# One chip kernel of three network blocks: chunk buffers cleared and gate rows split one stage earlier, woven pieces placed at lone steps, a head norm inverted on one tile, and attention probabilities scaled in their turn over

## The reference, cut to what matters

```python
# first block, diff_attention: 4 heads, 4 query blocks of 128
p = jax.nn.softmax(s, axis=-1)
p = p[:, :, 0] - lam * p[:, :, 1]
return jnp.einsum('bhqk,bkhd->bqhd', p, v)

# third block, gated_delta_rule, by chunks
lmat = jnp.where(strict, jnp.einsum('bhncd,bhnsd->bhncs', kb, k) * decay, 0.0)
sol = lax.linalg.triangular_solve(lmat + eye, rhs, left_side=True, lower=True, unit_diagonal=True)
value, k_cumdecay = sol[..., :dv], sol[..., dv:]
attn_intra = jnp.einsum('bhncd,bhnsd->bhncs', q, k) * decay
# a scan over the chunks with these follows, and then
o_gdn = rms_norm(o_gdn, gdn_norm_w) * jax.nn.silu(z)
gate = jax.nn.sigmoid(gates + gate_bias)          # gates: 2048 columns of h @ w_in
return (g_fox * y_fox + g_gdn * y_gdn) @ w_out
```

## Time and profile before

| | us |
|---|---|
| median of 3 runs | 2835.96 |
| lowest, highest | 2828.89, 2838.26 |
| the profiled execution | 2823.42 |
| its span | 2822.1 |
| TensorE busy in it | 2705.8 |

### The profile page before, as it was taken

One profiled execution on the slowest core, in us unless ns is written; L12 is line 12 of the kernel. 1 busy time (PEld: TensorE's weight loads), 2 busy tenths in 40 slices (PEclk: granted clock), 3 DMA queues, 4 the chain that ended last, 5 costly groups with the idle time before them and its releaser, 6 DMA issues. The chain is left out here.

```text
span 2822.1 us, 42499 instructions
## 1 busy us (share of the span) xinstructions
PE 2705.8 (96%) x16586; PEld 2320.4 (82%) x16586; DVE 1598.9 (57%) x2482; ACT 1053.2 (37%) x1827; POOL 642.0 (23%) x509
## 2 busy tenths in 40 slices
PE   8989999999999999998999999999899989999998
PEld 6769876788888777877888888986799889999987
DVE  5875657366653455954533337965544465666643
ACT  4364333442222333353423224546434243422223
POOL 3440101221100123441100003346344320112101
PEclk9999899999999999999999999999999999999999
DMA  4200231122222321312222222210111032222221
GB/s 163 92 8 8 91 104 60 46 90 97 97 97 97 117 75 62 103 38 74 92 97 97 97 97 76 87 50 1 51 35 46 28 120 85 88 91 91 97 98 60
DMA packets 64276, 219.08 MB, mean 78 GB/s; under 512 B 8182, under 2 KB 8822, under 8 KB 63830
## 3 DMA queue, kind: packets, MB, share of 16 engines
q1 hardware_dynamic: 61190, 211.62, 22.3%
q10 hardware_dynamic: 2896, 4.82, 0.5%
HBM read 210.07 MB, written 6.32 MB: 77 GB/s over the span
## 5 line engine op out<-in xcount | busy, mean ns | idle before, releaser
L308 PE MATMUL ps<-normed,slab_parts 128*128 128x512 f32 (+3 forms) x2280 | 789.8, 346 | 23.7 <-DVE normed L646 10.1
L310 PE MATMUL ps<-normed,slab_parts 128*128 128x512 f32 (+3 forms) x2280 | 767.8, 337 | 0.0
L309 PE MATMUL ps<-normed,slab_parts 128*128 128x512 f32 (+3 forms) x2280 | 767.3, 337 | 0.0
L163 ACT ACTIVATE slab_parts<-ring 128x1024 fp32r<-128x1024 f32 x360 | 380.1, 1057 | 893.3 <-PE ps L310 876.6
L167 DVE TENSOR_TENSOR slab_parts<-ring,slab_parts 128x1024 fp32r<-128x1024 f32 x344 | 461.5, 1344 | 380.7 <-ACT slab_parts L163 380.3
L308 PEld LDWEIGHTS ps<-normed,slab_parts 128*128 128x128 f32 x2280 | 434.3, 190 | 78.0 <-issue 20.0
L309 PEld LDWEIGHTS ps<-normed,slab_parts 128*128 128x128 f32 x2280 | 434.5, 191 | 47.3 <-issue 5.3
L310 PEld LDWEIGHTS ps<-normed,slab_parts 128*128 128x128 f32 x2280 | 433.7, 190 | 44.4
L308 PE MATMUL ps<-hidden,slab_parts 128*128 128x512 f32 x560 | 219.5, 392 | 5.6 <-DVE hidden L258 5.6
L310 PE MATMUL ps<-hidden,slab_parts 128*128 128x512 f32 x560 | 219.3, 392 | 0.0
L309 PE MATMUL ps<-hidden,slab_parts 128*128 128x512 f32 x560 | 219.3, 392 | 0.0
(11 more groups left out here) (602 smaller groups left out, 4351.1 us busy)
## 6 DMA issues: line engine op xcount, KB each, us to landing
ring<-in_stream SPq DMA_DIRECT2D x376, 512.0 KB, 3.3
scratch_gates<-fox_y SPq DMA_DIRECT2D x12, 258.0 KB, 2.3
branch_gates<-scratch_gates ACTq DMA_DIRECT2D x1, 2064.0 KB, 15.1
h<-in_x SPq DMA_DIRECT2D x8, 256.0 KB, 5.3
scratch_fox_y<-fox_y SPq DMA_DIRECT2D x1, 1032.0 KB, 6.8
gdn_z<-scratch_gates ACTq DMA_DIRECT2D x1, 1032.0 KB, 5.1
fox_y<-scratch_fox_y ACTq DMA_DIRECT2D x1, 1032.0 KB, 17.2
mix_y<-in_sgu_b SPq DMA_DIRECT2D x1, 1024.0 KB, 6.6
```

The costliest lines, as they stand in the source:

```text
L163: self.nc.scalar.activation(self.hi[:, n % PARTS, :], self.ring[:, n % SLOTS, :], ACT.Copy).then_inc(self.hi_ready, 1)
L308: nc.tensor.matmul(to, lhsT[0], rhs[0], start=start, stop=False)
L309: nc.tensor.matmul(to, lhsT[0], rhs[1], start=False, stop=False)
L310: return nc.tensor.matmul(to, lhsT[1], rhs[0], start=False, stop=stop)
```

## The change

**First attention.** GpSimd no longer scales probabilities. It multiplies the 128 by 128 identity by the inverse sums into `factors`, and TensorE turns each block over by a full matmul against it. As part 0 isn't scaled ahead of the join, the join's factor is now minus lambda times part 1's inverse sum times part 0's sum.

**Rates stage.** The chunk buffers (`ChunkRooms`) are allocated ahead of it and cleared in it by GpSimd, the masks are loaded in it, and ScalarE makes all eight high parts of `gate_rows` there, VectorE seven of the low ones; the eighth is the chunk stage's first VectorE operation. The warm-up products of the chunk stage are gone, as are the waits for cleared buffers. Pieces take the parts in the order 7, 4, 5, 0, 1, 2, 3, 6.

**Rooms.** A lone step takes 6 pieces at pairs or triangle and 3 otherwise; a step of two quads none with pairs or a result in it, 3 with a triangle, else 2. So 27 pieces stand ahead of quad 1's first pairs, where there were 6, and 20 in the last seven steps, where there were 10.

The diff, cut to its core:

```diff
-                        last = nc.tensor.transpose(turned_at(u, t), p[0:rows, u % KEEP, 0, t * rows:(t + 1) * rows], K.ident[0:rows, 0:rows])
+                        src = p[0:rows, u % KEEP, 0, t * rows:(t + 1) * rows]
+                        if parts == 2:
+                            last = nc.tensor.matmul(turned_at(u, t), src, factors[0:rows, u % KEEP, :], start=True, stop=True)
+                        else:
+                            last = nc.tensor.transpose(turned_at(u, t), src, K.ident[0:rows, 0:rows])
...
+                            ins = nc.vector.scalar_tensor_tensor(out=stat[0:rows, u % KEEP, 1, 3:4], in0=stat[0:rows, u % KEEP, 1, 3:4], scalar=minus_lambda[0:rows, :],
+                                                                 in1=stat[0:rows, u % KEEP, 0, 2:3], op0=ALU.mult, op1=ALU.mult)
...
-                    dve.wait_ge(p_scaled, u + 1)
+                    dve.wait_ge(inverted, parts * (u + 1))
...
-                    pool.wait_ge(inverted, parts * (u + 1))
+                    pool.wait_ge(inverted, parts * u + 1)
...
-                        nc.gpsimd.tensor_scalar(pp[:, 0, 0:keys], pp[:, 0, 0:keys], inv[:, 0, 3:4], None, ALU.mult).then_inc(p_scaled, 1)
+                        nc.gpsimd.tensor_scalar(factors[0:rows, u % KEEP, :], K.ident[0:rows, 0:rows], inv, None, ALU.mult).then_inc(spread, 1)
...
+        root = K.buf(local, "gdn_root_mean", [P, 2, TAIL // 2])
+        pick = K.buf(local, "gdn_pick", [P, 8, HD])
...
+        def factor_at(n):
+            return K.ps[:, 4 + (n + 2) % 4, 0:TAIL // 2]
...
-                    if t >= 2:
-                        pe.wait_ge(mean_out, t - 1)
                     for c, (lo, hi) in enumerate(cols.halves):
-                        last = nc.tensor.matmul(K.ps[:, 4 + 2 * (t % 2) + c, 0:hi - lo], K.blk, root[:, t, lo:hi], start=True, stop=True)
+                        last = nc.tensor.matmul(K.ps[32 * t:32 * (t + 1), 4 + c, 0:hi - lo], K.blk[:, HD - 16:HD + 16], square[:, t, lo:hi], start=True, stop=True)
                     last.then_inc(summed, 1)
...
+                def factors(n):
+                    t, c = divmod(n, 2)
+                    pe.wait_ge(picked, 1)
+                    pe.wait_ge(inverted, c + 1)
+                    if n >= 4:
+                        pe.wait_ge(normed, n - 3)
+                    nc.tensor.matmul(factor_at(n), pick[:, 2 * t:2 * t + 2, :].rearrange("p h m -> p (h m)"), root[:, c, :], start=True, stop=True).then_inc(spread, 1)
...
-                        sums(2 * i + 1)
+                    if i == 0:
+                        for t in range(4):
+                            sums(t)
+                    if APPLY <= i < APPLY + 2:
+                        for n in range(4):
+                            factors(4 * (i - APPLY) + n)
...
+                    if i == 0:
+                        act.wait_ge(mean_out, 1)
+                        nc.scalar.activation(root[:], root[:], ACT.Sqrt).then_inc(rooted, 1)
...
-                    for n in range(2 * (i - APPLY), 2 * (i - APPLY) + 2) if APPLY <= i < APPLY + 4 else ():
+                    if i == 0:
+                        dve.wait_ge(summed, 4)
+                        nc.vector.tensor_scalar(root[:], K.ps[:, 4:6, 0:TAIL // 2], 1.0 / HD, EPS, ALU.mult, ALU.add).then_inc(mean_out, 1)
+                    if i == 1:
+                        dve.wait_ge(rooted, 1)
+                        for c in range(2):
+                            nc.vector.reciprocal(root[:, c, :], root[:, c, :]).then_inc(inverted, 1)
+                    for n in range(4 * (i - APPLY), 4 * (i - APPLY) + 4) if APPLY <= i < APPLY + 2 else ():
                         t, (lo, hi) = n // 2, cols.halves[n % 2]
...
                         at = yg[:, t, FROM + lo:FROM + hi]
-                        nc.vector.scalar_tensor_tensor(out=at, in0=at, scalar=gain, in1=root[:, t, lo:hi], op0=ALU.mult, op1=ALU.mult).then_inc(normed, 1)
...
-                    nc.gpsimd.tensor_tensor(root[:, t, :], yg[:, t, FROM:T3], yg[:, t, FROM:T3], ALU.mult).then_inc(squared, 1)
+                    nc.gpsimd.tensor_tensor(square[:, t, :], yg[:, t, FROM:T3], yg[:, t, FROM:T3], ALU.mult).then_inc(squared, 1)
+                nc.gpsimd.tensor_copy(pick[:], K.ident[:, 0:P:16].unsqueeze(2).to_broadcast((P, 8, HD))).then_inc(picked, 1)
...
+        def low(dve, k):
+            dve.wait_ge(hi_ready, gate_rows.ORDER.index(k) + 1)
+            gate_rows.split_lo(k)
...
                 link(nc.vector.tensor_tensor(flat[:, 2, :], flat[:, 2, :], flat[:, 0, :], ALU.mult))
+                for k in (gate_rows.OWN_ROOM, *gate_rows.FREE_RATES):
+                    low(dve, k)
...
+                    if n % 2:
+                        dve.wait_ge(tiles_turned, 2 * i + 2)
+                        low(dve, gate_rows.VALUES[i])
...
+                for k in gate_rows.ORDER[0:3]:
+                    gate_rows.split_hi(k).then_inc(hi_ready, 1)
                 for n in range(len(lots)):
                     take(n)
+                    if 3 <= n < KT:
+                        gate_rows.split_hi(gate_rows.ORDER[n]).then_inc(hi_ready, 1)
...
-                for t in zeroed:
-                    nc.gpsimd.memset(t[HD:P], 0.0)
+                lower = [t[HD:P] for t in (*zeroed, *rooms.wides, *rooms.rhs)]
+                for t in lower:
+                    nc.gpsimd.memset(t, 0.0).then_inc(lower_cleared, 1)
+                pool.wait_ge(lower_cleared, len(lower))
+                for t in rooms.block_prod:
+                    nc.gpsimd.memset(t[:], 0.0)
...
+    OWN_ROOM, FREE_RATES, VALUES, LATE = 7, (4, 5), (0, 1, 2, 3), 6
+    ORDER = (OWN_ROOM, *FREE_RATES, *VALUES, LATE)
...
-        self.slot_of = [s for s in sorted(room) if s >= self.FIRST for _ in range(room[s])][:tiles * self.PIECES]
+        self.slot_of = [s for s in sorted(room) for _ in range(room[s])][:tiles * self.PIECES]
...
                 if i:
                     pe.wait_ge(self.drained, half - 1)
-            if half == 0:
-                pe.wait_ge(self.rows.lo_ready, k + 1)
+            if half == 0 and k == self.rows.LATE:
+                pe.wait_ge(self.late_ready, 1)
...
-        if slot < KT:
-            self.rows.split_hi(act, slot)
...
+    def vector_begin(self):
+        self.rows.split_lo(self.rows.LATE).then_inc(self.late_ready, 1)
...
-        if slot < KT:
-            self.rows.split_lo(dve, slot)
...
+    def __init__(self, K, ctx):
+        self.masks = K.buf(ctx, "gdn_masks", [C3, LEVELS_G + 5, C3])
+        self.wides = [K.buf(ctx, n, [P, 2, QUAD, C3]) for n in ("gdn_prod", "gdn_A_level", "gdn_inv", "gdn_invT")]
+        self.rhs = [K.buf(ctx, n, [P, 2, QUAD, HD]) for n in ("gdn_beta_v", "gdn_beta_k")]
+        self.block_prod = [K.buf(ctx, f"gdn_prod_{n}", [P, 2, QUAD, min(n, C3 - n)]) for n in (32, 64)]
...
-            room[slot - 1] = 2 + 2 * (TRIANGLE in steps) - 2 * (PAIRS in steps)
+            if len(steps) == 1:
+                room[slot - 1] = 6 if steps[0] in (PAIRS, TRIANGLE) else 3
+            else:
+                room[slot - 1] = 0 if PAIRS in steps or RESULT in steps else 3 if TRIANGLE in steps else 2
...

-                warm(K, 0, 4)
...

-                for t in wides + wide_rhs:
-                    nc.vector.memset(t[HD:P], 0.0).then_inc(padded, 1)
-                for t in block_prod:
-                    nc.vector.memset(t[:], 0.0).then_inc(padded, 1)
```

117 lines of the change are left out of this document (57 added, 60 removed).

## The result

The changed kernel's median is 2807.2 us in four runs (2805.4 to 2809.7), against 2832.4 for the kernel before in four. The ratio is 0.9913, with a 95% interval of 0.9895 to 0.9931. With more runs it was 0.9908 (0.9896 to 0.9921), medians 2807.0 and 2832.2. So the kernel is faster by 25 to 26 us. The forecast had the sign, and its range, 2806 to 2836, just holds the time, but the forecast gain of 15.4 us is six tenths of what came.

The account below looks back on a forecast made before the run. TensorE, busy 96% of the span, was taken to bound the kernel. The terms summed to −15.4 us, making the profiled 2823.4 us 2808 and the median 2820.6, range 2806 to 2836.

Parts of the forecast that it names:

- Lone start: Chunk stage, quad 0's pairs to quad 1's: 27 pieces in place of 6 with warm-ups and waits, +0.2 us.
- Lone end: Chunk stage's last seven steps: 20 pieces instead of 10, less 0.3 us falling into waits, +3.4 us.
- Two quads: Chunk stage's two-quad steps: two pieces fewer at result steps, −8.2 us; one fewer at triangle steps, −0.5 us.
- Scan: Scan's first matmuls, at half clock before: denser TensorE at the chunk stage's end wins half back, −0.9 us (0 to −1.8).
- Merge clock: Merge's start: with idle ahead cut from 4.25 to 1.8 us, the clock is less often at half, −1.5 us.
- Blocked lows: Rival, rates stage: GpSimd's memsets hold VectorE's low splits, stage ends 4 us later instead of 0.7; sum −12.1; chance 0.08.
- the attention's term: First attention: full matmuls add 4.4 us on TensorE, VectorE's 3.0 us wait for GpSimd goes; −1.0 us taken.
- inverse chain: Rival, chunk stage: each quad's inverse chain sets the pace, so 8.2 us comes back as idle; −7.2 us; chance 0.18.
- costlier turn over: Rival, first attention: a block costs over 0.7 us in place of 0.215; at 0.86, +25.8 us; chance 0.02.
- late y: Rival, chunk stage's start: pieces stall at the 17th, waiting for fox's y to be stored; +4 us; chance 0.03.
- half clock in the lone stretches: Rival: without warm-ups the clock falls at the chunk stage's start and end; sum +11.6 us, slower; chance 0.05.
- More than I count: Rival: triangle pieces, turn over, merge and attention all at their good ends, −20.5 us or less; chance 0.10.

Follow-up runs that it names:

- after2: The whole changed kernel, not edited further, timed in more rounds and profiled again: ratio 0.9908, median 2807.0 us.
- weave: The kernel before with only the change's rates stage, chunk stage and rooms: ratio 0.9965, −10 us.
- strip: The changed kernel with 16 more sum instructions, all to one strip of 32 rows, ahead of the gate stage's sums: gate stage 57.87 us.
- norm: The kernel before with only the change's head norm in the gate stage: ratio 0.9994, −2 us.
- attlight: The kernel before with the changed first attention, but plain transpositions in place of its full matmuls (result lacks a division): ratio 0.9961, median 9.6 us below before's.
- attfill: The kernel before with each of the first attention's 40 blocks turned over twice: ratio 0.9983, median 5.4 us below before's.
- headwarm: The changed kernel with the first attention of before and two warm-up matmuls at the start of the stage behind it: ratio 0.9926, median 2811.7 us.
- after: The first profiled execution of the whole changed kernel: span 2808.4 us.
- noatt: The changed kernel with the first attention left as before: ratio 0.9942, −16.4 us, median 2814.8 us.
- att: The kernel before with only the change's first attention: ratio 0.9980, −5.7 us.

## Why the prediction was right and wrong

**Right, with its size.** *Chunk start*: −4.8 forecast, −4.77 measured. *Lone start*: +0.2 forecast, +0.06. *Lone end*: +3.4 forecast, from 2212.59 to some 2229.3, 16.7 in place of 12.8, +3.9; the idle ahead of the scan grew too, from 0.80 to 1.26, which no term has. *Two quads and quad 1's turn over*: −1.2 −8.2 −0.5 = −9.9 forecast. From quad 1's first pairs to quad 0's last result it took 206.46 (2006.13 to 2212.59) in place of 217.65, −11.2: the turn over gave −0.7, and the result and triangle steps −10.5 where −8.7 stood. That is 31 pieces at 0.34 us each, so the triangle pieces were probably under-rated; the two kinds aren't told apart. The chunk stage as a whole, from its first TensorE instruction to the scan's, gave −11.5 where the terms give −11.1. *Merge idle*: 1.8 forecast, 1.80.

**Right in part by luck.** *Scan*: −0.9 forecast, −1.0 in the first pair. With the changed chunk stage it took 31.31 in all seven profiled executions; with the old one 32.3 in three and 31.31 in four, so on the mean the gain is less than half of that. *Merge clock*: −1.5 forecast. In the first pair the clock was full, 28 matmuls stood in 3.4 us in place of 16, worth 1.4 us, and the merge to the end was 0.9 shorter; but in five of the seven profiled executions with the changed gate stage the merge started at half clock after the same idle, and in after2 the merge to the end took 494.5, as in the first profile of before.

**Rates stage.** The +0.7 is right where the clock comes back early: 15.6 in weave, after2 and strip against 14.98 and 15.02 in before and norm. Where it comes back late, both take 18.7 to 18.8, and the change costs nothing. The +3.75 of the first pair is the clock's, at the same code: before itself has 14.98 and 18.70. *Blocked lows* fell: three lows took 2.09 us beside a memset, and the low that stood beside a GpSimd multiply took 1.32 in place of 0.75. The Trainium skill's page "SBUF — State Buffer" (SBUF: two separate sides) lets an operation with two SBUF inputs contend only with a GpSimd operation that reads SBUF, and both rows bear it out; the wider wording of "GPSIMD Engine Reference" (Specifications), two SBUF inputs without that limit, is not borne out by the first.

**The step that failed: the attention's term.** −1.0, bounds −3.0 and +1.5. It was made from waits inside the attention, and the edit measured −5.7 by the ratio alone (6.5 between the medians) and −7.8 between the medians on top of the rest. In profiled executions it gave 0.7 to 2 us in the attention and 1.2 behind it, against before's short executions; with the whole change the 1.6 of the stage behind the head norm took most of that back. What is left is the stage behind: 17.2 us in all four profiled executions with the full matmuls and in attlight, 18.3 to 25.9 in the eight with the attention of before or attfill's (headwarm's 21.05 includes its added matmuls), three of them above 23. In the terms of the prediction, TensorE's clock at that border was put at nothing. The forecast looked at the stage itself and not at what state TensorE leaves it in. It had priced an idle's effect on the clock for the chunk stage, the scan and the merge, and not for the border at 194.5 us, although the profile of before had the clock at half there too, at that stage's start:

```profile
194.50:198.00 3.50, 3.50 (x22) 3.10 (x23) 1.95 (x3) 2.44 (x5) 0.00 (x0) 0.65 0.00 0
```

**A second step: the sum carried over to the median.** "It ran 12.5 below the median; I take the difference over." The sum was made on an execution that was faster than all 29 later ones, with a clock that was back early in the rates stage and behind the attention. Behind the attention the change makes that regular; in the rates stage it doesn't (18.73 in after, 15.6 in after2). So the difference was not a constant to be carried over: after the change the profiled execution was 2.5 above the median. Of some 12 us between the gain of the profiled pair and that of the medians, 3 are the rates stage, early in the one and late in the other, and 6 to 8 the attention edit.

**A third, smaller: the sums in the gate stage.** "TensorE keeps 16 sum instructions" priced them at the old 3.1 us; in four strips they took 1.13. The stage term was −1.6; the stage shrank by 4.2 (57.16 to 52.94), and 2.0 of the difference is this. The other 0.6 isn't traced. The gate stage too has two values at the same code (57.16 and 58.70 before; 52.94 and 54.34 after), and it shrank by 4.2 to 4.4 from either.

**Of the rivals**, *inverse chain* is refuted by the waits of 5.1 us against 4.9, *costlier turn over* by 0.30 us a block, *late y* by a lone start that was busy for 16.20 of 16.20 us, and *half clock in the lone stretches* by the clock of 1.00 in both. The 0.86 a block of the costlier turn over was four times a transposition's 0.215. The Trainium skill's "FP8 and Floating Point Precision" (TensorE Precision Notes) states four passes for a true FP32 matmul, and no price against a transposition. So 0.30 against 0.195 speaks against the factor of four over a transposition, and says nothing against four passes. The chunk stage was the steadiest of all: 240.7 to 240.8 us in the seven profiled executions with the changed one, 252.2 to 252.3 in the seven with the old one, whatever happened elsewhere. *More than I count* was the nearest of them, and one of its four reasons happened, the dearer triangle pieces; the turn over gave 0.7, the merge's clock 1.4 at most, and the attention's gain lay behind the attention and not in its waits.

**What stays open.** Whether the wait for GpSimd alone does it: the traces of attlight and attfill say so, with one execution each, and the gain of attfill's median has no explanation. What brings the clock back early or late at the same code, behind the attention and in the rates stage, is not known. And the parts don't add up: noatt and att, −16.4 and −5.7, give −22.1, where after2 has −26, inside the intervals; but weave, norm and att, −10, −2 and −5.7, give some −17, and the 9 us to −26 are a little more than the intervals allow together.

## What to carry to other kernels

Where TensorE waits in small pieces at a stage's end, price what its clock will be in the stage behind, over several executions: the value of taking such waits away is in the executions that one profile doesn't show. Before adding terms to a profiled execution, see where its time stands among the runs (its mean granted clock alone didn't tell here) and compare stage lengths over more than one profile of each kernel: here the scan and the merge of the first pair looked like gains that other executions didn't repeat. A spread of 17 us is itself something that a change can take away. And pieces of real work in place of warm-up matmuls cost next to nothing where TensorE was waiting for a chain, and take their full length out of a stretch where it is busy.
